# Value projection of a memory moved out of attention and retention to the ends of two blocks, key projection cut finer

## The reference, cut to what matters

```python
# first block (context ctx, conditioning c)
qa_x, ka_x, va_x, qr_x, kr_x, vr_x, gr_x = project(hx, w_in, ...)
att_x = latent_attention(...)            # 8 heads, softmax over 512 keys
ret_x = bidir_retention(...)             # 8 heads, two directions
mix_x = merge_heads(att_x, ret_x, gr_x, w_out)
x_new = x + gt_m * rms_norm(mix_x, g_post_mix)
hf = modulate(rms_norm(x_new, g_pre_ffn), sh_f, sc_f)
x_new = x_new + gt_f * rms_norm(swiglu(hf, w_ffn_in, w_ffn_out), g_post_ffn)
# second block
x = x + 0.5 * swiglu_2(rms_norm_2(x, ffn1_norm), ffn1_gate, ffn1_up, ffn1_down)
# ... a gated recurrence with a convolution ...
mn = rms_norm_2(mem, mem_norm)
kv = mn @ w_kv_mem                       # 256 x 2048: keys km and values vm
p = softmax(einsum(qm, km) * MEM_HD ** -0.5)
att = einsum(p, vm)
```

## Time and profile before

| | |
|---|---|
| median of 3 runs | 1124.44 us (1123.78 to 1125.28) |
| profiled execution, its time | 1123.16 us |
| its span | 1121.3 us |
| TensorE busy | 1044.1 us (93%) |
| VectorE, ScalarE busy | 604.4 us (54%), 491.3 us (44%) |
| DMA | 188.71 MB, mean 168 GB/s |
| chain that ended last | PE 87%, DVE 5%, DMA 3%, ACT 3% |

### The profile page before, as it was taken

How to read it: one execution, slowest core, us unless ns; L and a number is a source line. 1 busy time by engine, 2 the same in 40 slices (tenths; PEclk the granted TensorE clock), 3 DMA queues, 4 the chain that set the end, 5 groups by cost and what they waited for, 6 DMA issues and landing times.

```text
span 1121.3 us, 13376 instructions
## 1 busy us (share of the span) xinstructions
PE 1044.1 (93%) x5212; PEld 846.3 (75%) x5212; DVE 604.4 (54%) x708; ACT 491.3 (44%) x581; POOL 0.2 (0%) x4
## 2 busy tenths in 40 slices
PE   4799999999699999989999999899889789999996
PEld 1578768787588888868888887688777677888885
DVE  1672854567655555455555545746654436555543
ACT  3352444545444444345444434653345336444431
POOL 0000000000000000000000000000000000000000
PEclk9799999999899999999999999899999999999999
DMA  9666654223255555536545455433224325554540
GB/s 378 265 258 226 233 217 151 76 76 113 75 188 187 187 186 189 188 113 243 180 166 197 178 199 199 180 120 113 79 108 153 113 75 188 178 197 169 187 169 37
DMA packets 26542, 188.71 MB, mean 168 GB/s; under 512 B 2944, under 2 KB 3200, under 8 KB 3968
## 3 DMA queue, kind: packets, MB, share of 16 engines
q1 hardware_dynamic: 25920, 185.63, 45.6%
q10 hardware_dynamic: 576, 2.43, 0.6%
HBM read 187.00 MB, written 1.05 MB: 168 GB/s over the span
## 4 chain that ended last, share of the span: by engine, by line
PE 87%; DVE 5%; DMA 3%; ACT 3%; issue 1%; SPq 0%; DVEq 0%; ACTq 0%
PE bank L1640 25%; PE bank L1642 24%; PE bank L1641 24%; DMA raw<-in_weights 3%; PE bank L1707 2%; PE bank L1696 1%; PE bank L1870 1%; PE bank L1979 1%; PE bank L1859 1%; DVE w_lo L1042 1%; ACT w_hi L577 1%; PE bank L2063 1%; PE bank L2153 1%; PE bank L2162 1%; PE bank L1908 1%
## 5 line engine op out<-in xcount | busy, mean ns | idle before, releaser
L1042 DVE TENSOR_TENSOR w_lo<-raw,w_hi 128x2048 fp32r<-128x2048 f32 (+1 forms) x153 | 339.2, 2220 | 276.1 <-ACT w_hi L577 276.0
L577 ACT ACTIVATE w_hi<-raw 128x2048 fp32r<-128x2048 f32 x148 | 282.9, 1915 | 283.2 <-PE bank L1642 253.9
L1640 PE MATMUL bank<-w_hi,hT_hi 128*128 128x512 f32 (+1 forms) x864 | 344.4, 399 | 11.6 <-DVE w_lo L1042 5.0
L1641 PE MATMUL bank<-w_lo,hT_hi 128*128 128x512 f32 (+1 forms) x864 | 337.8, 391 | 0.0
L1642 PE MATMUL bank<-w_hi,hT_lo 128*128 128x512 f32 (+1 forms) x864 | 337.7, 391 | 0.0
L1640 PEld LDWEIGHTS bank<-w_hi,hT_hi 128*128 128x128 f32 x864 | 164.2, 190 | 53.7 <-issue 9.8
L1642 PEld LDWEIGHTS bank<-w_hi,hT_lo 128*128 128x128 f32 x864 | 164.2, 190 | 34.9
L1641 PEld LDWEIGHTS bank<-w_lo,hT_hi 128*128 128x128 f32 x864 | 164.6, 191 | 32.1
L1640 PE MATMUL bank<-w_hi,gT_hi 128*128 128x512 f32 x264 | 103.3, 391 | 0.0
L1642 PE MATMUL bank<-w_hi,gT_lo 128*128 128x512 f32 x264 | 102.8, 389 | 0.0
L1641 PE MATMUL bank<-w_lo,gT_hi 128*128 128x512 f32 x264 | 102.7, 389 | 0.0
(11 more groups left out here) (261 smaller groups left out, 1009.6 us busy)
## 6 DMA issues: line engine op xcount, KB each, us to landing
raw<-in_weights SPq DMA_DIRECT2D x172, 1024.0 KB, 4.8
arena<-in_const ACTq DMA_DIRECT2D x1, 1088.0 KB, 5.0
x_res<-in_x SPq DMA_DIRECT2D x1, 1024.0 KB, 8.4
arena<-in_ctx SPq DMA_DIRECT2D x1, 1024.0 KB, 9.9
memKT<-in_mem SPq DMA_DIRECT2D x1, 1024.0 KB, 10.3
out<-xn SPq DMA_DIRECT2D x2, 512.0 KB, 2.7
arena<-in_const SPq DMA_DIRECT2D x1, 770.0 KB, 6.3
rows<-in_final_norm ACTq DMA_DIRECT2D x1, 512.0 KB, 5.0
```

What stands on the lines that cost most here:

```text
L577: act.activation(w_hi[:, v_slot, :], raw[:, u_slot, :], ACT.Copy).then_inc(hi_ready, 1)
L1042: ins = dve.tensor_tensor(w_lo[:, v_slot, n], raw[:, u_slot, n], w_hi[:, v_slot, n].bitcast(F32), ALU.subtract)
L1640: pe.matmul(out, hi, rhi, start=start, stop=False)
L1641: pe.matmul(out, hi, rlo, start=False, stop=False)
```

## The change

The value projection is taken out of the filling. `W_KV` keeps the four key units. The value units are renumbered `W_V[0]` (two units, behind `W_OUT`) and `W_V[1]` (two units, behind block 0's down units).

- Attention: filling is counted in triples, one behind the scores and two behind the previous weighted sum. Retention: two in every head. 16 x 3 + 8 x 2 = 64 key triples.
- End of the mixer: 13 value triples before the transposes of block 0's input and 3 behind them. End of block 0: 8 before the transposes of block 1's input and 8 behind.
- The tables of splits shrink: the steps split three units instead of five and the heads one instead of three, and the copies of the keys go to steps 6 and 11, head 2 and behind the heads.
- ScalarE and VectorE split both value units before `post_norm`, and the first unit of the next block inside the norm: ScalarE behind `post_norm`; VectorE behind scaling (block 0) or behind the residual sum (block 1).
- The gains' rows now lie in `memV`, whose halves are overwritten by the values after their last use, since `rows` shares its place with the high part of the transposed memory.
- Banks of the keys, of the values and of the two sets of transposes are others.

```diff
-W_OUT = W_KV + 8
-W_UP = [W_OUT + 4, 0, 0]
+W_OUT = W_KV + 4
+W_V = [W_OUT + 4, 0]
+W_UP = [W_V[0] + 2, 0, 0]
 W_DN = [W_UP[0] + 2 * UP, 0, 0]
-W_UP[1] = W_DN[0] + UP
+W_V[1] = W_DN[0] + UP
+W_UP[1] = W_V[1] + 2
...
-STEP_QUANTA = 5
-HEAD_QUANTA = {0: 8, 1: 8, 3: 8, 4: 8, 5: 8, 6: 8}
-KEY_STEPS = {4: 0, 7: 1, 10: 2, 13: 3}
-HIGH_STEPS = {0: W_KV + 2, 4: W_KV + 3, 7: W_KV + 4, 10: W_KV + 5, 13: W_KV + 6}
...
-LOW_HEADS = {2: W_KV + 7, 4: W_OUT, 6: W_OUT + 1}
+BEHIND_SCORES, BEHIND_WEIGHTED = 1, 2
+HEAD_QUANTA = 2
+KEY_STEPS = {6: 0, 11: 1}
+HIGH_STEPS = {0: W_KV + 2, 6: W_KV + 3, 11: W_OUT}
...
+LOW_HEADS = {2: W_OUT + 1}
+VALUES_AHEAD = (13, 8)
...
+        gain_row = lambda g, c: memV[:, c, g * 512:(g + 1) * 512]
...
-            split_to(W_OUT + 5)
+            split_to(W_V[0] + 2)
...
+            split_to(W_UP[0] + 1)
             norm_stats(x, x_added(("mix_out",), 0))
             norm_scale(x, xn)
-            split_to(W_OUT + 4 + 2)
+            split_to(W_UP[0] + 2)
             split_T("ffn0T", shifted=True)
+            split_to(W_UP[0] + 3)
+            values_out(0)
             ffn(0)
-            split_to(W_UP[1] + 2)
+            split_to(W_V[1] + 2)
             post_norm(("down", 0), 1)
+            split_to(W_UP[1] + 1)
             pre_norm("ffn1T", x_added(("down", 0), 0), col("ffn1_norm"), W_UP[1])
+            values_out(1)
...
-            low_to(W_OUT + 5)
+            low_to(W_V[0] + 2)
...
-                low_to(dn + UP + 1)
+                low_to(dn + UP)
...
             post_norm(y_mix, ("mix_out",), 0)
             norm_stats(x, x_added(("mix_out",), 1))
             norm_scale(x, xn)
+            low_to(W_UP[0] + 1)
             split_T("ffn0T", shift=(a_ffn, mod[:, 24:32, 0]))
+            low_to(W_UP[0] + 3)
             ffn(0)
+            low_to(W_V[1] + 2)
             post_norm(y_ffn, ("down", 0), 1)
+            low_to(W_UP[1] + 1)
...
+            def value_products(c):
...
+                for half in range(2):
+                    v = W_V[c] + half
+                    pe.wait_ge(split_ready, v + 1)
+                    outs = [(free(pe, ("memV", c, tb)) if half == 0 else bank_of(("memV", c, tb))) for tb in range(TB)]
+                    for tb in range(TB):
...
+                        for e in range(4):
...
+                            ins = three(outs[tb][:, :], memT_hi[:, k, t], memT_lo[:, k, t], w_hi[:, v % RING, w],
+                                        w_lo[:, v % RING, w], k == 0, k == KC - 1)
+                            if tb == 1 and e == 3:
+                                ins.then_inc(split_used, 1)
+                            yield
...
                 if s + 2 < 2 * HEADS:
                     scores(s + 2)
+                fill(BEHIND_SCORES)
                 if s:
                     weighted(s - 1)
-                fill(STEP_QUANTA)
+                fill(BEHIND_WEIGHTED)
...
                     retention_scores(r + 1)
-                fill(HEAD_QUANTA.get(r, 0))
+                fill(HEAD_QUANTA)
                 retained(r)
...
+            values = value_products(0)
+            take(values, VALUES_AHEAD[0])
             transpose_input("ffn0T", xn)
+            take(values, 16 - VALUES_AHEAD[0])
             ffn(0, "ffn0T")
+            values = value_products(1)
+            take(values, VALUES_AHEAD[1])
             transpose_x("ffn1T", added(("down", 0)))
+            take(values, 16 - VALUES_AHEAD[1])
             ffn(1, "ffn1T")
```

More of the change, by code:

```diff
@@ L208, in ffn, with four_transposes, values @@
                 plan.streamed(("down", f, tb, half), tb * 2 + half)
-    def four_transposes(stage):
-        for q in range(4):
-            plan.signalled((stage, q), 4 + q)
+    def four_transposes(stage, banks=(4, 5, 6, 7)):
+        for q, b in enumerate(banks):
+            plan.signalled((stage, q), b)
+    def values(c, banks):
+        for tb in range(TB):
+            plan.streamed(("memV", c, tb), banks[tb])
     plan.streamed(("mod_row", 0), 7)
@@ L247, in plan_banks @@
     for u in range(4):
-        plan.streamed(("memK", u), [6, 3][u % 2])
-    for c in range(2):
-        for tb in range(TB):
-            plan.streamed(("memV", c, tb), 6 + tb)
+        plan.streamed(("memK", u), 6 + u % 2)
     plan.streamed(("att", 0), 4)
@@ L2015, in ffn, with take @@
                     down(k)
+            def take(products, n):
+                for _ in range(n):
+                    next(products)
+            values = value_products(0)
+            take(values, VALUES_AHEAD[0])
             transpose_input("ffn0T", xn)
+            take(values, 16 - VALUES_AHEAD[0])
             ffn(0, "ffn0T")
+            values = value_products(1)
+            take(values, VALUES_AHEAD[1])
             transpose_x("ffn1T", added(("down", 0)))
+            take(values, 16 - VALUES_AHEAD[1])
             ffn(1, "ffn1T")
@@ L2219, in lay_out @@
     w_kv = f("w_kv_mem_2")[0]
-    w += [whole(w_kv[:, c:c + 256]) for c in range(0, D, 256)] + project(w_kv[:, D:])
+    w += [whole(w_kv[:, c:c + 256]) for c in range(0, D, 256)]
+    values = project(w_kv[:, D:])
     w_out = f("w_out")[0]
```

66 lines of the change are left out of this document (29 added, 37 removed).

## The result

| | before | after |
|---|---|---|
| median of 4 runs each | 1124.86 us (1123.78 to 1129.12) | 1108.1 us (1107.32 to 1109.1) |
| profiled execution, its time | 1123.16 us | 1107.32 us |
| its span | 1121.3 us | 1105.5 us |
| TensorE busy | 1044.1 us (93%) | 1037.3 us (94%) |
| mean granted clock | 0.977 | 0.984 |

The ratio is 0.9854 with a 95% interval of 0.9831 to 0.9876: the changed kernel is 1.5% faster. The forecast was 1107.6 us. In what follows a stage's length is the distance between two starts of TensorE, read in the profiled execution of each kernel, and the last column is the forecast of the prediction's sum.

What follows compares the result with a forecast made beforehand. TensorE was taken as the bound, with two holes at the norms. Terms -12.9 - 8.4 + 1.2 - 0.4 + 4.9 = -15.6 us, from the profiled 1123.2, gave 1107.6 us (range 1102 to 1116, chance 0.66).

Steps and rivals of the forecast that it cites:

- What bounds the kernel: Whole run: TensorE busy 93%, its time full stretches plus two holes at the norms, longest waits 8.1 and 3.7 us.
- Prices of 0.68 and 0.36 us a triple: TensorE's product triples: 0.68 us for one of 512 columns (values), 0.36 us for one of 256 columns (keys).
- Attention, -12.9: Attention's 16 steps: fewer triples -11.2, covered waits -1.2 and -0.7, late copies +0.2; net -12.9 us (bounds -6 and -13.5).
- Retention, -8.4: Eight retention heads: products -10.7, waits for VectorE 3.3 where 1.0 were; net -8.4 us (bounds -10.7 and -5).
- Head norm, +1.2: Norm after retention: VectorE's low part ends 1.2 us later against the mixer's first output product; +1.2 us (bounds 0 and +2).
- End of the mixer, -0.4: Up to block 0's start: 16 value triples absorbed, transposes at full clock; -0.4 us (bounds -2.5 and +4).
- End of block 0, +4.9: Up to block 1's start: hole smaller than the 16 triples put in; +4.9 us (bounds +3.5 and +8).
- A: Attention and retention bound by ScalarE and VectorE: attention gives half its cut (-6.5), retention -6; 1116.4 us, chance 0.09.
- B: Both norms start 4.2 us late behind an extra high and low part; 1114.4 us, chance 0.08.
- C: Short holes in almost every retention head make TensorE's clock fall there; 1131.6 us, chance 0.05.
- D: VectorE keeps up in retention and at the head norm (-2.3, -1.2); 1104.1 us, chance 0.10.
- E: The edit gives nothing, new waits equal the filled ones; 1123 us, chance 0.02.

Runs made afterwards that it cites:

- experiment 6: Changed kernel with all three key triples of an attention step behind the weighted sum instead of one ahead and two behind: 1109.56 us, ratio 0.9856.
- experiment 10: Changed kernel with 12 of the 16 key triples of each key unit left out, in attention and retention: 1096.02 us, ratio 0.9764.
- experiment 3: Changed kernel with the two key triples of the last retention head done in head 6 instead: 1105.0 us, ratio 0.9822.
- experiment 4: Changed kernel with retention's 16 key triples spread by where TensorE waited (1, 1, 3, 4, 4, 0, 3, 0) instead of two per head: 1102.52 us, ratio 0.9813.
- experiment 1: Changed kernel with all 16 value triples of the mixer's end behind the transposes of block 0's input, none ahead: 1115.55 us, ratio 0.9934.
- experiment 8: Kernel before the change with 13 dummy triples added ahead of the transposes of block 0's input: 1124.75 us against 1124.13, ratio 1.001.
- experiment 7: Changed kernel with the low part of block 0's first weight unit made over 64 columns instead of 2048: 1105.78 us, ratio 0.9831.
- experiment 5: Changed kernel with 12 of the 16 value triples at block 0's end left out: 1103.36 us, ratio 0.9816.
- experiment 2: Changed kernel with all 16 value triples of block 0's end ahead of the transposes instead of 8: 1108.8 us, ratio 0.9872.
- experiment 9: Kernel of experiment 4 with the low part of block 0's first weight unit made by GpSimd instead of VectorE: 1106.83 us, ratio 0.9847.

## Why the prediction was right

*What bounds the kernel.* Right in what matters. The work removed is none and the time fell by what the two gaps took in, less what they couldn't. One reading is wrong: 3.7 us was not the second longest single wait behind the start. In the second block TensorE waits longer, once, at 712.71 us, for a low part:

```profile
PE bank L1640 <- DVE w_lo L1042: 5.0, 1, 5.0
```

The change leaves this wait as it is (4.96 us at 696.88), so the sum doesn't suffer; but it is a larger hole than the one at block 0's end.

*Prices of 0.68 and 0.36 us a triple.* Right: they give the attention step of 3.3 us (3.25 measured), and the 9.00 busy of 9.00 us in the former hole.

*Attention, -12.9.* Measured -13.35. Its two parts hold by themselves: the moved triple was to save 1.9 us, and experiment 6 puts it back at +2.20. The reserve in ScalarE's and VectorE's waits was real, and experiment 10 shows where it ends. The 0.45 us beyond the forecast I can't assign to a row.

*Retention, -8.4.* Measured -9.37. The waits were named in the right four heads and for the right reason (experiments 3 and 4 make them vanish by covering them), but they were mis-sized. By the lengths of the heads they cost 2.8 us where 3.3 stood in the sum (their rows say 0.32, 0.55, 0.58 and 0.32, 1.8 together, against 0.5, 1.1, 1.3 and 0.5). And the one wait before cost more than the 1.0 of its row: that head took 3.94 us (239.68 to 243.62), where scores and retained products alone take 2.46, so 1.5. The products came off as forecast: four value triples had taken 2.92 to 2.96 us, two key triples take 0.90, which makes -10.6 for the stage. With +1.3 for the waits instead of +2.3 that is -9.3. For head 3 the count had the masked scores ready 14.0 us behind the stage's start and TensorE at 13.0; in the trace it is 13.76 and about 13.3. VectorE's operations start before the one ahead ends (2.20 us from the low part to the next, where 2.29 was added), and TensorE had lost 0.6 us in head 2. This term is the largest miss of the sum, 1.0 us.

*Head norm, +1.2.* Measured +1.30, and by the named mechanism: the low part begins 1.30 us later against the output product, and experiment 3 takes all of it away.

*End of the mixer, -0.4.* Measured +0.82 by the stage, less the 1.5 us that block 0's first products had lost to the half-rate clock: -0.7. Each step of it is in the trace: 13 triples to 282.98 with no wait, transposes in 1.91, the low part in front of the shift, a wait of 1.75 (about 2 was said). Experiment 1 shows the price of the hole, 8.9 us, experiment 8 that the clock's loss was 1.5, experiment 7 that the low part's place costs 0.77. The 1.5 us of the clock rest on stage lengths, and the whole time of experiment 8 doesn't bear them out.

*End of block 0, +4.9.* Measured +3.42 with the clock's 1.5 in it: +4.9. Experiment 5 confirms the reason, a hole smaller than the work put in: of 8.2 us removed only 3.3 come back.

*The total.* The sum was -15.6, the stages say -17.15 and the span -15.8: the 1.5 us by which the sum was too cautious (1.0 retention, 0.45 attention, 0.3 at the mixer's end, less 0.1 at the head norm) met a start that happened to be 1.35 us later. The base was lucky too: it was the profiled execution's 1123.16, and from the median before, 1124.86, the same sum gives 1109.3. So 1107.6 against 1108.1 is closer than the working deserves.

*The rivals.* A (attention gives half its cut) is refuted by -13.35 and by experiment 10: there, of the next 13 us, 65% still come off in attention, and half of the cut in retention. B (a norm late behind its low part) is refuted: no wait ahead of either set of transposes. C, the clock that falls in retention, is refuted by the window 216 to 246: TensorE busy for 28.24 of 30 us and granted 1.00, with a wait in four of eight heads. By the rule of the Trainium skill that stood behind it (TensorE: Matmul & The Clock Gate, "A second HAM failure mode: psum-queue depth-cycling") the short idle moments would have made the clock swing; the trace disagrees for gaps of 0.3 to 0.6 us. D (VectorE keeps up) isn't what the change did, but experiments 3 and 4 show that it needed only another distribution of the same products. E is refuted by the ratio.

## What to carry to other kernels

A wait of TensorE at a norm can take in products that depend on nothing nearby, and it then also keeps the clock at full, but only products that stand in front of the wait do it (experiment 1), and only as many as the gap is long (experiment 5). Leave a few for behind the transposes, where the other engines need time to split the result (experiment 2), and look where the last filling of the old place occupies a ring slot that the next stage needs (experiment 3). When filling is thinned out, place what remains at the heads or steps that wait, not evenly: with the ring slot freed by it, that was worth 4.1 us of 1108 (experiment 4).

## What the runs showed of the hardware that I had not expected

- A GpSimd operation of 5.12 us stretched a VectorE operation from 1.23 to 5.38 us (experiment 9). Two engines that share no data can still run one after the other.
- Stage lengths in the middle of the program repeat to about 0.02 us between kernels and chips (attention 57.91 to 57.93 us in eight kernels), with one exception of 0.5 us in attention's first step (experiment 8). The start of the program, which waits for its first weights, varies from 155.9 to 158.4 us, and the part behind block 1's output from 433.8 to 435.3. An effect of 1 us is seen in a stage when the medians of five runs don't show it.
- The idle time in a wait's row is less than what the wait costs: four heads with 1.8 us of it were 2.8 us longer than heads without.
- Half-rate transposes cost little by themselves: they take 1.8 us longer, but the stretch from them to block 0's start is only 0.5 us longer (5.45 against 4.94 us in experiment 8). The first tiles arrive late, and from there VectorE's work on the tiles ends the stretch in either case (4.31 us from the shift's start to block 0's at half rate, 4.30 at full).
